# Paged decode's values as plain fp32 products of 8 columns in four column groups, with a weight ring of 16

## What is computed

```python
def fox_sample(q, k_new, v_new, logf_new, k_past, v_past, logf_past):
    ...
    sp = (jnp.einsum('bqhd,bkhd->bhqk', q, k_past).astype(F32) * scale
          + cn[..., None] + r_excl[:, :, None, :])
    ...
    return (jnp.einsum('bhqk,bkhd->bqhd', p[..., :P], v_past)
            + jnp.einsum('bhqk,bkhd->bqhd', p[..., P:], v_new))
```

## Time and profile before

| | |
|---|---|
| median of 3 runs | 2845.83 us (2845.45 to 2847.18) |
| the profiled execution | 2846.01 us, its span 2844.1 us |
| PE | 2739.7 us busy (96%), 13712 matmul instructions |
| DVE, ACT, POOL | 1594.3, 1028.4 and 752.0 us busy |
| granted TensorE clock, mean | 0.989 |

### The profile page before, as it was taken

How to read it: one execution, slowest core, us unless ns; L and a number is a source line. 1 busy time by engine, 2 the same in 40 slices (tenths; PEclk the granted TensorE clock), 3 DMA queues, 4 the chain that set the end, 5 groups by cost and what they waited for, 6 DMA issues and landing times.

```text
span 2844.1 us, 38365 instructions
## 1 busy us (share of the span) xinstructions
PE 2739.7 (96%) x13712; PEld 2245.9 (79%) x13712; DVE 1594.3 (56%) x3067; ACT 1028.4 (36%) x1952; POOL 752.0 (26%) x688
## 2 busy tenths in 40 slices
PE   7999998999999999899999999999999988999998
PEld 6778777777778888787778778878778877888886
DVE  7414477443342676875566666656664754554545
ACT  2211111433332454452445455545543332323322
POOL 5148775044225352533010060020020232000000
PEclk9999999999999999999999999999999999999999
DMA  5677779656546666657664475355445564332331
GB/s 185 256 257 230 227 249 308 205 182 195 176 158 233 224 223 226 219 188 228 226 184 145 142 237 169 115 177 174 129 136 191 204 215 152 114 123 101 123 118 55
DMA packets 292075, 525.96 MB, mean 185 GB/s; under 512 B 111486, under 2 KB 120255, under 8 KB 270639
## 3 DMA queue, kind: packets, MB, share of 16 engines
q1 hardware_dynamic: 233247, 314.60, 35.3%
q10 hardware_dynamic: 56880, 204.34, 20.8%
q0 software_dynamic: 1760, 4.59, 0.5%
HBM read 411.02 MB, written 112.41 MB: 184 GB/s over the span
## 4 chain that ended last, share of the span: by engine, by line
PE 73%; POOL 6%; DVE 6%; DMA 4%; issue 3%; SPq 2%; ACT 1%; ACTq 0%; DVEq 0%; POOLq 0%
PE fill_out L2715 23%; PE fox_o_sum L381 4%; PE fox_turned L427 4%; PE in_out L100 4%; PE in_out L101 4%; PE in_out L102 4%; PE mf_out L100 3%; PE mf_out L102 3%; PE mf_out L101 3%; POOL dc_slot L1719 2%; PE fox_scores L415 2%; PE mf_fin L100 2%; PE mf_fin L102 2%; PE mf_fin L101 2%; PE fox_scores L416 2%
## 5 line engine op out<-in xcount | busy, mean ns | idle before, releaser
L2715 PE MATMUL fill_out<-keep_hi,fill_x 128*128 128x512 f32 x1488 | 513.1, 407 | 5.7 <-POOL keep_lo L2825 3.7
L2715 PEld LDWEIGHTS fill_out<-keep_hi,fill_x 128*128 128x128 f32 x1488 | 272.4, 190 | 53.6 <-POOL keep_lo L2825 5.0
L2715 PE MATMUL fill_out<-keep_lo,fill_x 128*128 128x512 f32 x744 | 302.4, 407 | 0.0
L536 DVE TENSOR_TENSOR fox_pt_lo<-fox_turned,fox_pt_hi 128x512 fp32r<-128x512 f32 (+1 forms) x320 | 194.7, 608 | 159.0 <-ACT fox_pt_hi L479 156.5
L479 ACT ACTIVATE fox_pt_hi<-fox_turned 128x512 fp32r<-128x512 f32 (+1 forms) x320 | 170.2, 532 | 305.1 <-PE fox_turned L427 302.3
L2309 ACT ACTIVATE in_stage<-in_out 128x512 f32<-128x512 f32 (+1 forms) x119 | 70.9, 597 | 552.3 <-PE in_out L102 509.7
L522 DVE CUSTOM_DVE_ANT_0 fox_probs<-fox_scores,fox_bias 128x512 f32<-128x512 f32 (+2 forms) x320 | 186.9, 606 | 91.6 <-PE fox_scores L416 60.3
L2816 POOL CAST keep_hi<-fill_raw 128x512 fp32r<-128x512 f32 x72 | 48.9, 679 | 708.6 <-PE fill_out L2725 690.4
L2715 PE MATMUL fill_out<-keep_hi,hg_fill_x 128*128 128x512 f32 x624 | 215.1, 407 | 6.8 <-POOL keep_lo L2825 5.4
L427 PE MATMUL fox_turned<-ident,fox_probs 128*128 128x128 f32 x1088 | 172.4, 274 | 8.4 <-ACT fox_probs L470 7.3
L2715 PEld LDWEIGHTS fill_out<-keep_lo,fill_x 128*128 128x128 f32 x744 | 141.2, 190 | 22.4
(11 more groups left out here) (422 smaller groups left out, 6747.4 us busy)
## 6 DMA issues: line engine op xcount, KB each, us to landing
fill_x<-x_tiles ACTq DMA_DIRECT2D x91, 1024.0 KB, 6.0
hg_fill_x<-x_tiles ACTq DMA_DIRECT2D x38, 1024.0 KB, 5.4
dc_slot<-in_cache_fox_k_dram SPq DMA_DIRECT2D x128, 256.0 KB, 3.6
dc_slot<-in_cache_fox_v_dram SPq DMA_DIRECT2D x128, 256.0 KB, 3.4
in_raw<-in_w_in_dram SPq DMA_DIRECT2D x104, 256.0 KB, 4.0
plain<-fill_stage ACTq DMA_DIRECT2D x96, 256.0 KB, 5.1
turned<-in_stage ACTq DMA_DIRECT2D x64, 256.0 KB, 4.0
fill_raw<-in_w_in_dram SPq DMA_DIRECT2D x56, 256.0 KB, 2.7
```

The lines of the kernel that those rows point to most:

```text
L536: dve.tensor_tensor(pt_lo[:, b, skip:BANK], bank_of(st)[:, skip:BANK], pt_hi[:, b, skip:BANK].bitcast(F32), ALU.subtract).then_inc(turned_ ...
L2715: ins = pe.matmul(self.out[n % self.OUTS][:], x, w, start=(k == 0 and term == 0), stop=(ends and term == 2))
```

## The change

- A value product is now a plain fp32 one: the stationary tile is the page's probabilities as they are, 128 x 8 (128 x 4 for memory), the moving tile is the page in its slot, 128 x 512. Nothing is rounded or split on ACT or DVE, and `dc_pr`, `low` and `lows` are gone.
- Two tasks of the paged cache make a set (`set_of`) of four pages. Page `part` of a set writes to partitions 32 x `part` and up of the row's bank, so the four products use four groups of 32 columns of the array. A memory task is a set by itself, of two pages. PE does a set one tick after its last task's tick.
- `copy_row` adds the four (two) parts: one copy and three (one) adds of 8 x 512 (4 x 512).
- A slot is free when PE has multiplied (`valued`); SP's reload for the paged and memory values moves to `free_tick`, two ticks after the set's last task.
- PE waits for the exponentials and for the slots' loads itself.
- The weight ring has all 16 places in every pass, and the last group's splits no longer wait for decode's end.

```diff
-    GP, SLOTS, QS, RING = 2, 4, 3, 2
+    GP, SLOTS, QS = 2, 4, 3
...
+    def set_of(self, n):
+
+        return [n] if n >= self.K + self.PAGED else [n - (n - self.K) % 2, n - (n - self.K) % 2 + 1]
+
+    def free_tick(self, n):
+
+        return self.tick_of(n) + 1 if n < self.K else self.tick_of(self.set_of(n)[-1]) + 2
...
         if before >= self.K:
-            eng.wait_ge(self.lo_ready, 2 * (before - self.K) + 2)
+            eng.wait_ge(self.valued, before - self.K + 1)
...
-            if t == self.tick_of(n - self.SLOTS) + 1:
+            if t == self.free_tick(n - self.SLOTS):
                 self.load_slot(sp, n)
...
-    def low(self, dve, n):
...
     def copy_row(self, dve, r):
         a, n = r // B, self.last_of_row(r)
+        row, bank, heads = self.row[r % 2][0:self.heads[a]], self.bank_of_row(r), self.heads[a]
+        parts = self.GP * len(self.set_of(self.K + n))
         dve.wait_ge(self.valued, n + 1)
         if r >= 2:
             dve.wait_ge(self.row_stored[r % 2], 16 * (r // 2))
-        dve.tensor_copy(self.row[r % 2][0:2 * self.heads[a]], self.bank_of_row(r)[0:2 * self.heads[a], :]
-                        ).then_inc(self.row_copied, 1)
...
+        self.link(dve.tensor_copy(row, bank[0:heads, :]))
+        for part in range(1, parts):
+            ins = dve.tensor_tensor(row, bank[part * LINE:part * LINE + heads, :], row, ALU.add)
+            if part < parts - 1:
+                self.link(ins)
+        ins.then_inc(self.row_copied, 1)
...
-        for n in self.tasks_at(t, self.K, 2 * self.K):
-            a, b, g = self.tasks[n - self.K]
-            v = n - self.K
-            act.wait_ge(self.exp_ready, a + 1)
-            if v >= self.RING:
-                act.wait_ge(self.valued, v - self.RING + 1)
...
         for n in self.tasks_at(t - 1, self.K, 2 * self.K):
-            self.values(pe, n)
+            if n == self.set_of(n)[-1]:
+                self.values(pe, n)
...
-        pe.wait_ge(self.lo_ready, 2 * v + 2)
-        for p in range(self.GP):
-            weights = self.pr[v % self.RING][:, p, :]
-            pe.matmul(bank[0:SAMPLE_COLUMNS, :], weights, self.v_hi[v % self.RING][:, p, :],
-                      start=(v == self.first_of_row(r) and p == 0), stop=False)
-            m = pe.matmul(bank[0:SAMPLE_COLUMNS, :], weights, self.v_lo[v % self.RING][:, p, :], start=False,
-                          stop=(v == self.last_of_row(r) and p == self.GP - 1))
-        m.then_inc(self.valued, 1)
+        pe.wait_ge(self.exp_ready, r // B + 1)
+        for m in some:
+            pe.wait_ge(self.loaded[m % self.SLOTS], 16 * self.GP * (m // self.SLOTS + 1))
+        for part in range(self.GP * len(some)):
+            m, p = some[part // self.GP], part % self.GP
+            a, b, g = self.tasks[m - self.K]
+            last = pe.matmul(bank[part * LINE:part * LINE + heads, :], self.scores[a][:, b, g * self.GP + p, :],
+                             self.slot[m % self.SLOTS][:, p, :], start=first, stop=n - self.K == self.last_of_row(r))
+        last.then_inc(self.valued, len(some))
...
-    VALUES = RING_SLICES - Decode.RING * Decode.GP
+    VALUES = RING_SLICES
...
-            if m >= LOADS * KT and ring_at[m] >= VALUES:
-                eng.wait_ge(decode.valued, decode.K)
```

More of the change, by code:

```diff
@@ L1523, in __init__ @@
         self.slot = [sb(f"slot{s}", [P, GP, W]) for s in range(self.SLOTS)]
[L1524 to L1527, removed]
         self.q = [sb(f"q{i}", [P, 1, W]) for i in range(self.QS)]
-        self.row = [sb(f"row{i}", [2 * FH, W]) for i in range(2)]
-        self.o_hi, self.o_lo, self.z = small_rows[0:3]
+        self.row = [sb(f"row{i}", [FH, W]) for i in range(2)]
+        self.o, self.z = small_rows[0:2]
         self.ones, self.later = sb("ones", [P, P]), sb("later", [P, P])
@@ L1551, in __init__ @@
         self.suffix_all = small[:, at:at + FH]
-        self.o_dram = [nc.dram_tensor(f"dc_o_rows{a}", (B, (2 * self.heads[a] + 1) * W), F32, kind="Internal").ap()
+        self.o_dram = [nc.dram_tensor(f"dc_o_rows{a}", (B, (self.heads[a] + 1) * W), F32, kind="Internal").ap()
                        for a in range(2)]
@@ L1674, in load_rows @@
             sp.dma_start(self.z[:], self.rows.row_of("mz")).then_inc(self.z_loaded, 16)
[L1675 to L1678, removed]
+        own = self.o_dram[a][:, 0:heads * (W + dim)].rearrange("b (h x) -> b h x", h=heads)[:, :, 0:dim]
+        sp.dma_start(self.o[:].rearrange("b (h d) -> b h d", h=heads), own).then_inc(self.o_loaded, 16)
     def sync_end(self, sp):
@@ L1689, in gpsimd @@
             link(pool.memset(self.ones[:], 1.0))
-            for pr in self.pr:
-                link(pool.memset(pr[:].bitcast(F32), 0.0))
             link(pool.memset(self.later[:], 1.0))
@@ L1711, in gpsimd @@
                 pool.wait_ge(self.row_copied, r + 1)
-                pool.dma_start(self.o_dram[a][b:b + 1, 0:2 * self.heads[a] * W].rearrange("o (h n) -> (o h) n", n=W),
-                               self.row[r % 2][0:2 * self.heads[a]]).then_inc(self.row_stored[r % 2], 16)
+                pool.dma_start(self.o_dram[a][b:b + 1, 0:self.heads[a] * W].rearrange("o (h n) -> (o h) n", n=W),
+                               self.row[r % 2][0:self.heads[a]]).then_inc(self.row_stored[r % 2], 16)
     def multiply(self, eng, n, signal):
@@ L1774, in vector @@
             if t == self.end_tick(a) + 4:
[L1775 removed]
+                dve.wait_ge(self.o_loaded, 16 * (a + 1))
                 if a == 0:
[L1777 removed]
+                    dve.sem_inc(self.o_ready, 1)
                 else:
[L1779 to L1780 removed]
+                    by_head = self.o[:].rearrange("b (h d) -> b h d", d=HD)
                     link(dve.tensor_tensor(by_head, by_head, self.inverse[:].unsqueeze(2).to_broadcast([B, HH, HD]), ALU.mult))
                     dve.wait_ge(self.z_loaded, 16)
[L1783 removed]
+                    dve.tensor_tensor(self.o[:], self.o[:], self.z[:], ALU.mult).then_inc(self.o_ready, 1)
     def middle(self, dve, a, m):
@@ L1828, in scalar @@
                 act.activation(self.scores[a][:], self.scores[a][:], ACT.Exp).then_inc(self.exp_ready, 1)
-        for n in self.tasks_at(t, self.K, 2 * self.K):
-            a, b, g = self.tasks[n - self.K]
-            v = n - self.K
-            act.wait_ge(self.exp_ready, a + 1)
-            if v >= self.RING:
-                act.wait_ge(self.valued, v - self.RING + 1)
-            act.activation(self.pr[v % self.RING][:, :, 0:self.heads[a]],
-                           self.scores[a][:, b, g * self.GP:(g + 1) * self.GP, :], ACT.Copy).then_inc(self.hi_ready, 1)
-            act.wait_ge(self.loaded[n % self.SLOTS], 16 * self.GP * (n // self.SLOTS + 1))
-            if v < self.RING:
-                self.values_free(act)
-            act.activation(self.v_hi[v % self.RING][:], self.slot[n % self.SLOTS][:], ACT.Copy
-                           ).then_inc(self.hi_ready, 1)
     def tensor(self, pe, t):
@@ L1875, in tensor @@
         for n in self.tasks_at(t - 1, self.K, 2 * self.K):
-            self.values(pe, n)
+            if n == self.set_of(n)[-1]:
+                self.values(pe, n)
     def values(self, pe, n):
-        v, r = n - self.K, self.row_of(n)
-        bank = self.bank_of_row(r)
-        if v == self.first_of_row(r):
+        some, r = self.set_of(n), self.row_of(n)
+        first, bank, heads = some[0] - self.K == self.first_of_row(r), self.bank_of_row(r), self.heads[r // B]
+        if first:
             if r >= B + 3:
@@ L2154, in project_and_decode @@
         recur = RecurSample(nc, core, ctx, small, small_rows, extra, sums, lb_param, state_in, gain, gated, state_out)
-        def values_free(eng):
-            last = max(m for m in range(G * KT) if ring_at[m] >= VALUES) // KT
-            eng.wait_ge(out_ready, event_at[last, U - 1] + 1)
         decode = Decode(nc, core, ctx, small, wide, extra, small_rows, sums, recur, page_table, logf_pages, paged, cached,
-                        past_o, past_stat, gated, w_ring.keep, values_free)
+                        past_o, past_stat, gated)
         forget = ForgetGates(nc, core, ctx, x_both, xs_both, x_loaded, small, extra, tall_rows, sums, recur, decode,
```

16 lines of the change are left out of this document (3 added, 13 removed).

## The result

The changed kernel takes 2815.26 us, the median of four runs (2813.63 to 2817.14), against 2846.51 us for the kernel before in the same comparison. The ratio is 0.9888, 95% interval 0.9873 to 0.9903: faster by 31 us, 1.1%. The forecast was 2853 us, slower by 7; the time lies 7 us above rival A (2808 us).

The account below looks back on a forecast made before the run. PE was taken to bound the kernel, busy 2739.7 of 2844.1 us. 79.1 + 4 - 67.0 - 8 - 1.1 = +7.0 us on about 2846 us gave 2853 us, range 2801 to 2870 us.

Parts of the forecast that it names:

- rival A: Value products on PE: all four column groups run at once, values cost 34.4 + 4 us, total 2808 us; chance 0.31.
- value products removed: PE's value line: 288 fp32r products at 0.2325 us each go away, 67.0 us less.
- plain fp32 products added: PE's value line: 144 products in 40 sets, 2.15 us per four pages, 1.29 per two, 79.1 us more.
- going in and out: PE switching between 128-column and eight-column products: 0.1 us a set taken, 4 us; bounds 0 to 9.6 us.
- ring of 16: Weight ring: PE's stalls on POOL's weight splits and the slow clock after them go, 8 us less.
- splits gone: ACT's and DVE's splits of values: worth only PE's one wait for them, 1.1 us less.
- Part 2: Plain fp32 products added to PE: 79.1 us, from program order hiding one half of each page after the first.
- the two bounds: Cost of PE's added products: 123.8 us without any overlap, 34.4 us with all column groups at once.
- The unit prices: PE: 0.2325 us per fp32r product; 0.43 us per plain fp32 instruction at 512 columns, 0.86 a product.
- Rival D: Weight ring: stalls stay because they came from SP being late, not the ring; +8 us, 2861 us; chance 0.05.
- Part 6: SP's reloads and PE's new waits for slot loads: about 3 us of cover, costed at nothing.
- rival C: New slot waits or returning weight stalls on PE: +10 to 15 us on the forecast, 2863 to 2868 us; chance 0.07.

Follow-up runs that it names:

- a0: The changed kernel itself, run again on one chip with the ring-of-12 kernels: 2814.44 us, 0.9888 of the kernel before.
- e11: Changed kernel with only 12 of the weight ring's 16 places from the seventh load on, repeated on the changed kernel's chip: 2821.97 us, 0.9912 of before.
- e12: Changed kernel with ring of 12 and unused value splits put back, slot reloads waiting for them, repeated on the changed kernel's chip: 2828.04 us, 0.9931 of before.
- e2: Changed kernel with paged sets in two column groups, pages 0 and 1 in one, 2 and 3 in the other: 2845.68 us, one run.
- e3: Changed kernel with paged sets in two alternating column groups, pages 0 and 2 in one, 1 and 3 in the other: 2847.22 us, one run.
- e1: Changed kernel with all pages of a set in one column group: 2907.12 us, one run, against 2844.85 before.
- e6: Changed kernel with ring of 12 and unused value splits put back, slot reloads waiting for them, first comparison: 2826.14 us, 0.9915 of before.
- e8: Changed kernel with paged sets of four tasks, eight pages, two products in each of four groups: 2822.66 us, 0.9915 of before.
- e7: Changed kernel with every task a set by itself, paged sets of two pages instead of four: 2847.75 us, 0.9994 of before.
- e4: Changed kernel with every set's products issued twice in a row into the same bank: 2853.54 us, one run, against 2844.85 before.

## Why the prediction was wrong, point by point

| term | forecast, us | measured, us |
|---|---|---|
| value products removed | -67.0 | -71.4, all sets of before read as in the experiments, with their waits and slow clock |
| plain fp32 products added | +79.1 | 40 x 0.86 = +34.4 |
| going in and out | +4 | 37 x 0.31 = +11.5 |
| ring of 16 | -8 | -7.5 by medians (a0 against e11), -4.4 in the stage |
| splits gone | -1.1 | -6.1 by medians (e11 against e12), -4.8 and -8.3 in the stage |
| whole change | +7.0 | -32.3 (a0 against before) |

The measured terms overlap, since the 71.4 us hold waits that ring and splits are charged with, and are not to be added up.

**The step that failed** is Part 2's choice between the two bounds: it took strict program order across column groups as binding and gave a set of four pages 2.15 us of products, where the runs show 0.86. The reason given was that PE's rows never leave program order and the halves of one product stand together. The rows were no evidence: none of those shown for the kernel before has products in different column groups side by side, so that nothing in them could pass anything. e2 shows that an instruction for a free group passes those that wait for a busy one, and e3 that the order then does not matter. That is 79.1 - 34.4 = 44.7 us, more than the whole miss of 38 us. Rival A named the mechanism, with a chance of 0.31, and its 34.4 us for the products held.

**The unit prices held.** 0.43 us for a half of a product at 512 columns was doubled from 256; e1 shows 0.430. The 0.2325 us of an fp32r product held too: four take 0.93 us and eight 1.86 in most of the sets of before.

**The ring's term** of 8 us agrees with 7.5 by the medians, and that is partly luck. It stood for four stalls behind POOL's splits (5.3 us) and the slow clock after two of them (2.4 us). With the ring undone, 1.3 us of such waits came back in either profile, and 4.4 us in the stage, of which some 1.7 are a slow clock that is not tied to the ring. Rival D fits in part: most of the old stalls needed more than the smaller ring. With the splits back as well 2.2 us of waits for POOL are there (1.4 in e6), not 5.0; where the rest came from is open.

**Going in and out** was mis-sized: 0.1 us a set forecast, at most 0.24 as a bound, 0.31 measured. The earlier trace rows was read for the way out only; the row just ahead of it has the way in as well:

```profile
541.44 0.39 PE L102 MATMUL in_out<-rest_lo,x_first 128*128 128x512 f32 x1
```

From there to 541.76 us are 0.32 us where 0.227 is due, as in the value sets. So this place of the kernel before had 0.09 + 0.12 = 0.21 us, 8 us in 40 sets. The choice of 4 rested on loads ahead for both ways, and the changed kernel's do not come ahead: the weights of the next large product start loading at 525.79 us, 0.52 us after the last value instruction's start. Adjacent memory sets share one way in and out, hence 37 and not 40. Eight columns alone do not make the price. The kernel before also has eight instructions of eight columns that are transposes:

```profile
469.16 0.39 PE L102 MATMUL in_out<-rest_lo,x_first 128*128 128x512 f32 x1
...
469.39 1.03 PE L1862 MATMUL in_wide<-ident,dc_most 128*8 128x128 f32 x8
...
470.49 0.40 PE L101 MATMUL in_out<-rest_hi,x_first 128*128 128x512 f32 x1
```

They stand 0.11 us apart and cost nothing beside that: 1.33 us in all, less 0.454, is 0.88. What makes the difference was not tested.
The Trainium skill has a rule that TensorE drains when the tiling mode changes (TensorEngine Tiling (Array Packing), Key Properties). The 0.31 us is of the kind that such a drain would cost, but no run here shows that it is one.

**The splits** were priced by the one wait that the profile put down to them, 1.1 us, and the rest at nothing. The runs show 5 to 8 us. Behind the wait for `dc_sums`, PE's waits in the stage rise from 2.0 us in e11 to 6.3 in e12, and they are for slots, a row's copy and POOL's splits of weights, none of them for the splits of values by name. The rows had pointed there, since SP's issues headed the chain of the earlier trace rows, and that was used for the ring alone.

**The new waits** (Part 6, rival C) did not come: the changed kernel has none for a slot. That the cover is small fits e8: with eight issues in place of four in the same two ticks it waited 8.5 us for slots.

By medians the steps from before are -18.7 us to the ring of 12 with splits, -6.1 for the splits and -7.5 for the ring; that they add up to -32.3 follows from how they are made. The first step is the product's form alone, and -67.0 + 34.4 + 11.5 = -21.1 us is its sum from unit prices, 2 us from it. In the stage it is -20.7 us with e12 and -24.0 with e6.

The Trainium skill's model for tiles, in TensorE: Matmul & The Clock Gate, Part 3 (Measured speedup vs the span model), is one matmul's time plus some 4 ns for each further tile. This trace is close to it: the first four instructions of a set, one to a group, take 0.62 us together where one takes 0.60, so 0.02 us for three further groups, some 7 ns each.
The Trainium skill says in the same Part 3, under The mechanism, that matmuls start and end in program order. That does not hold for e2, where group 1's first instruction starts beside group 0's first, though four instructions of group 0 stand ahead of it. The measurement decides.

## What to carry to other kernels

Small stationary tiles pay where several of them can stand in different column groups at once: price such a batch as the longest group plus, in this kernel, 0.31 us for going in and out, and fill all four groups, since two pages cost what four do (1.16 and 1.17 us). When the trace cannot show an overlap, a run that puts the same products into one group settles it in one comparison; program order of work that could not overlap is no evidence on it. And when a term is undone by a run, compare the stage it touches as well as the whole: here the ring was 4.4 us in its stage and 7.5 by the medians. And work that PE never waits for by name can still be worth microseconds through the buffers and queues it holds.

## What the runs showed of the hardware that was not expected

- PE's column groups take plain fp32 instructions from the queue out of program order across groups: in e2 the fifth instruction of the set starts within 0.1 us of the first, and the eight take 1.90 us, not the 3.2 of strict order.
- Plain fp32 at 512 moving columns is 0.43 us a half, 0.86 us a product, with 8 columns as with 4; four products in four groups take 0.86 us, and so do two in two groups (1.17 and 1.16 us with going in and out).
- A batch of these eight-column products among large ones costs some 0.3 us beside its products, whether it holds four (e7), eight or sixteen instructions (e4, e8), in one, two or four groups. Eight transposes of eight columns in the kernel before cost nothing beside their 0.11 us each.
